# Late heads' pair parts, a third low part and the second norm's adds in other places

## What is computed

```
h = rms_norm(x);  z = h @ w_in     # pool 512 | q 512 | k 128 | v 128 | gate_pool 1024 | gate_attn 1024
yA = pool_mixer(z_pool) @ w_branch_pool
yB = window_attention(z_q, z_k, z_v) @ w_branch_attn
x = x + (sigmoid(gate_pool) * yA + sigmoid(gate_attn) * yB) @ w_out
h2 = rms_norm(x);  q = h2 @ w_q    # 8 heads, each with two halves of 128
s1, s2 = q_half1 . keys_1, q_half2 . keys_2       # top 16 of 128 each
cand = v1[i] + v2[j]               # top 16 of the 256 pairs, e_idx = i1 * 128 + i2
x = x + sum over the 8 * 16 chosen experts; out = rms_norm(x)
```

## Time and profile before

| | |
|---|---|
| time before, median of 3 runs | 2916.48 us (2912.46 to 2918.59) |
| the profiled execution's own time | 2923.75 us |
| its span, first to last instruction | 2921.7 us |
| mean granted TensorE clock | 0.984 of full speed |
| busy: PE, PEld, DVE, ACT, POOL | 95%, 83%, 82%, 32%, 72% |
| TensorE's wait for a weight tile's low part, whole mixer | 16.1 us in 9 waits, the longest 7.4 us |

### The profile page before, as it was taken

How to read it: one execution, slowest core, us unless ns; L and a number is a source line. 1 busy time by engine, 2 the same in 40 slices (tenths; PEclk the granted TensorE clock), 3 DMA queues, 4 the chain that set the end, 5 groups by cost and what they waited for, 6 DMA issues and landing times.

```text
span 2921.7 us, 39464 instructions
## 1 busy us (share of the span) xinstructions
PE 2785.8 (95%) x14843; PEld 2420.2 (83%) x14843; DVE 2406.7 (82%) x4433; ACT 935.6 (32%) x1366; POOL 2116.6 (72%) x1542
## 2 busy tenths in 40 slices
PE   8999999989997999999999999999999999999995
PEld 6688777677887888889989988999888889988995
DVE  2622797654799995889999999998999999999998
ACT  4422443323322995222222222222222222222222
POOL 5444477385686997788778886888777688878885
PEclk9999999999998999999999999999999999999998
DMA  4123422123322778889989988999889799989996
GB/s 154 49 87 99 162 61 84 44 87 108 104 90 102 236 234 283 314 327 349 337 310 352 348 307 322 346 337 351 313 318 344 283 347 346 329 317 348 337 343 218
DMA packets 267725, 717.87 MB, mean 246 GB/s; under 512 B 20880, under 2 KB 104208, under 8 KB 267536
## 3 DMA queue, kind: packets, MB, share of 16 engines
q0 software_dynamic: 110912, 403.75, 36.8%
q1 hardware_dynamic: 156624, 311.61, 31.7%
HBM read 657.86 MB, written 57.41 MB: 245 GB/s over the span
## 4 chain that ended last, share of the span: by engine, by line
DVE 20%; PE 20%; DMA 7%; issue 7%; POOL 5%; ACT 1%; DVEq 0%; POOLq 0%; SPq 0%; ACTq 0%
DVE acc L1883 9%; DVE e_y L1939 4%; DMA up<-in_down,e_idx 4%; PE ybank L1728 3%; PE abank L1712 3%; PE abank L1713 3%; PE abank L1714 3%; PE ybank L1729 3%; PE ybank L1730 3%; DVE up L1871 3%; DMA up<-in_up,e_idx 3%; POOL tdown_lo L1660 2%; DVE w_lo L1932 2%; POOL up L1653 2%; DVE w L1928 2%
## 5 line engine op out<-in xcount | busy, mean ns | idle before, releaser
L1712 PE MATMUL abank<-m_hT,tdown_hi 128*128 128x384 f32 (+1 forms) x1856 | 577.3, 311 | 4.7 <-PEq L1359 2.5
L1714 PE MATMUL abank<-m_hT,tdown_lo 128*128 128x384 f32 (+1 forms) x1856 | 577.5, 311 | 0.0
L1713 PE MATMUL abank<-m_hlo,tdown_hi 128*128 128x384 f32 (+1 forms) x1856 | 576.7, 311 | 0.0
L1728 PE MATMUL ybank<-tup_hi,w_hi 128*128 128x512 f32 x1280 | 506.8, 396 | 46.4 <-DVE e_y L1939 29.0
L941 POOL TENSOR_TENSOR m_wlo<-m_raw,m_whi 128x1024 fp32r<-128x1024 f32 x128 | 312.4, 2448 | 306.7 <-ACT m_whi L719 303.2
L1883 DVE SCALAR_TENSOR_TENSOR acc<-up,e_act,acc 128x1024 f32<-128x1024 f32 x381 | 489.5, 1285 | 43.7 <-DMA up<-in_up,e_idx 16.4
L1871 DVE CUSTOM_DVE_ANT_0 up<-up,acc 128x1024 f32<-128x1024 f32 x384 | 453.1, 1212 | 71.7 <-DMA up<-in_down,e_idx 62.4
L1729 PE MATMUL ybank<-tup_lo,w_hi 128*128 128x512 f32 x1280 | 504.5, 394 | 0.0
L1730 PE MATMUL ybank<-tup_hi,w_lo 128*128 128x512 f32 x1280 | 504.1, 394 | 0.0
L1653 POOL DMA_INDIRECT up<-in_up,e_idx x384 | 396.6, 1033 | 106.7 <-issue 88.9
L1653 POOL DMA_INDIRECT up<-in_down,e_idx x384 | 402.3, 1048 | 98.0 <-issue 73.7
(11 more groups left out here) (241 smaller groups left out, 4566.9 us busy)
## 6 DMA issues: line engine op xcount, KB each, us to landing
e_tup<-in_up SPq DMA_DIRECT2D x128, 512.0 KB
m_raw<-in_tiles SPq DMA_DIRECT2D x116, 512.0 KB, 3.5
e_tdown<-in_downT SPq DMA_DIRECT2D x116, 512.0 KB
gates<-all_table SPq DMA_DIRECT2D x64, 640.0 KB
all_table<-t_out SPq DMA_DIRECT2D x9, 4096.0 KB, 14.7
m_raw<-in_downT SPq DMA_DIRECT2D x12, 512.0 KB, 3.7
up<-in_down,e_idx POOLq DMA_INDIRECT x384
up<-in_up,e_idx POOLq DMA_INDIRECT x384
```

The lines of the kernel that those rows point to most:

```text
L1712: nc.tensor.matmul(out, tdown_hi[:, q, at], h2T_hi[:, k, a:b], start=k == 0, stop=False)
L1713: nc.tensor.matmul(out, tdown_hi[:, q, at], h2T_lo[:, a:b, at], start=False, stop=False)
L1714: ins = nc.tensor.matmul(out, tdown_lo[:, q, at], h2T_hi[:, k, a:b], start=False, stop=k == KD - 1)
L1728: nc.tensor.matmul(out, w_hi[r][:, q, ts], tup_hi[r][:, q, ds], start=q == 0, stop=False)
```

## The change

It is one of order alone: no computation is added or dropped.

- In the merge, `top_pairs` of a late head comes ahead of block m's low part (now `merge_low(m)`), except at m = 0. Heads 6 and 7 move from m = 3 and 5 to m = 4 and 6. `LOOKUPS` has one lookup for each m; the last one, (7, 1), comes behind the merge and the low parts of "out" 2 to 4.
- On GpSimd, at the end of the first group, the low part of the second group's third tile comes ahead of head 3's lookups, the fourth's between the two, the fifth's inside the second one, behind its multiply.
- In the second norm, of both groups, VectorE's adds of blocks 1, 2 and 3 move ahead of norm steps of the blocks before them.

```diff
-LATE = {0: 4, 2: 5, 3: 6, 5: 7}
+LATE = {0: 4, 2: 5, 4: 6, 6: 7}
-LOOKUPS = {1: ((4, 0),), 2: ((4, 1),), 3: ((5, 0), (5, 1)), 4: ((6, 0),), 5: ((6, 1),), 6: ((7, 0),), 7: ((7, 1),)}
+LOOKUPS = {1: (4, 0), 2: (4, 1), 3: (5, 0), 4: (5, 1), 5: (6, 0), 6: (6, 1), 7: (7, 0)}
...
-            def choose(g, hd, i):
+            def choose(g, hd, i, between=None):
...
                 link(nc.gpsimd.tensor_tensor(hit, hit, itopf[:, i].unsqueeze(2)
                                              .to_broadcast([P, TT, TOPK, TOPK]), ALU.mult))
+                if between is not None:
+                    tile_low(between)
                 for n in (8, 4, 2, 1):
...
                     if g and m in LOOKUPS:
-                        for hd, i in LOOKUPS[m]:
-                            choose(g - 1, hd, i)
+                        choose(g - 1, *LOOKUPS[m])
...
+                if g:
+                    through("out", 4)
+                    choose(g - 1, PH - 1, 1)
                 through("pq", 2)
...
-                    for hd in range(FIRST_LATE):
+                    for hd in range(FIRST_LATE - 1):
                         choose(g, hd, 0)
                         tile_low(min(first + NTILE + RING, made[0] + 1))
                         choose(g, hd, 1)
                         tile_low(min(first + NTILE + RING, made[0] + 2))
+
+                    tile_low(first + NTILE + RING)
+                    choose(g, FIRST_LATE - 1, 0)
+                    tile_low(first + NTILE + RING + 1)
+                    choose(g, FIRST_LATE - 1, 1, between=first + NTILE + RING + 2)
...
+                def merge_low(m):
+                    dve.wait_ge(m_high, g * KD + m + 1)
+                    nc.vector.tensor_tensor(mlo[:, m], sg[:, m % 2, 0], mhi(m).bitcast(F32), ALU.subtract).then_inc(m_low, 1)
...
                     nc.vector.tensor_tensor(sg[:, m % 2, 0], sg[:, m % 2, 0], sg[:, m % 2, 1], ALU.add).then_inc(merged, 1)
-                    dve.wait_ge(m_high, g * KD + m + 1)
-                    nc.vector.tensor_tensor(mlo[:, m], sg[:, m % 2, 0], mhi(m).bitcast(F32), ALU.subtract).then_inc(m_low, 1)
+                    if m == 0:
+                        merge_low(0)
                     if g and m in LATE:
...
                         top_pairs(g - 1, LATE[m], vlate[i], ilate[i], hits_late)
+                    if m:
+                        merge_low(m)
...
-                for t in range(TT):
-                    if t:
-                        finish_norm(t - 1)
+                def add_mixed(t):
                     for n in range(2):
...
-                    norm_start(g, 1, (t,))
-                finish_norm(TT - 1)
+
+                add_mixed(0)
+                add_mixed(1)
+                norm_start(g, 1, (0,))
+                finish_norm(0)
+                norm_start(g, 1, (1,))
+                add_mixed(2)
+                finish_norm(1)
+                norm_start(g, 1, (2,))
+                finish_norm(2)
+                add_mixed(3)
+                norm_start(g, 1, (3,))
+                finish_norm(3)
```

## The result

The changed kernel takes **2899.34 us** (median of 4 runs, 2896.84 to 2901.48), where the kernel before, in 4 runs between them, took 2916.05 (2912.46 to 2918.59). The ratio is 0.9943, with a 95% interval of 0.9926 to 0.9961. The difference of the medians is 16.7 us.

What follows compares the result with a forecast made beforehand. VectorE's selection bounds the mixer and starts as early as TensorE delivers, so gaps won before 751 us count. Terms sum to -14.2, 2923.75 to about 2909.6; less 7.3 to the median, 2902 us, range 2896 to 2906.

Steps and rivals of the forecast that it cites:

- first group's norm: Second norm, first group: VectorE's adds move ahead of earlier blocks' norm steps, last scaling starts earlier: -3.1 us.
- VectorE's held operation: Last early head's tail: VectorE's L1150 must wait out GpSimd's third low part, delaying the second group's first product: +2.35 us.
- clock behind it: TensorE's clock falls behind each new wait, at the second group's first product and in the output product: +2.5 us each.
- third tile's wait: Second group's pool products: TensorE no longer waits for the third low part, made in GpSimd's idle stretch: -7.3 us.
- the merge's stall: Merge: the round of 26.35 us shrinks to 16.74 with pair parts ahead of the low part, clock included: -9.6 us.
- output tile 2's wait: Output product: TensorE's gap for a low part goes, the lookup there being over before tile 2 is wanted: -1.3 us.
- the new wait in the output product: Output product: TensorE waits for a bank freed by block 7's add, now behind head 7's pair part: +3.9 us.
- second group's norm: Second norm, second group: the same 3.0 us earlier plus 1.1 of clock: -4.1 us.
- (a): Both new waits: the clock doesn't fall there; -19.2 us, 2897; kept with the forecast, together chance 0.64.
- (b): Neither new wait arises, VectorE slips between GpSimd's operations; -25.4 us, 2891; chance 0.16.
- (c): Merge: pair part doesn't come early, a gate tile still waits once, the 9.6 stays; -4.6 us, 2912; chance 0.13.
- (d): Merge: ScalarE's sigmoid waits for the later low part, starving TensorE behind heads 5, 6 and 7; +8.3 us, 2925; chance 0.05.

Runs made afterwards that it cites:

- e1_norm: The kernel before with the second norm's new order alone: 2907.97 us, ratio 0.9965.
- e3_merge: The kernel before with the merge's part alone (pair parts ahead of the low part, heads 6 and 7 moved, one lookup a round): 2910.88 us, ratio 0.9972.
- e5_lowwait: The changed kernel with GpSimd waiting for the turned blocks' first low part before making the third low part: 2899.28 us, ratio 0.9941 to the kernel before.
- e9_after_again: The changed kernel measured again, nothing altered: 2899.87 us, ratio 0.9949 to the kernel before.
- e11_lowwait_again: Repeat of the changed kernel whose third low part on GpSimd waits for the turned blocks' first low part: 2901.00 us, ratio 0.9936 to the kernel before.
- e7_order: The kernel before with the pair part ahead of the merge's low part alone, heads and lookups at their old places: 2912.80 us, one run.
- e6_both: The changed kernel with GpSimd's third low part waiting and head 7's pair part behind the add of m = 7: 2893.73 us, ratio 0.9916 to the kernel before.
- the two halves: The kernel before with the merge part's order alone, 2912.80 us, and with its new places of heads and lookups alone, 2916.17 us.
- e2_third: The kernel before with the third, fourth and fifth low parts moved alone: 2911.07 us, ratio 0.9972.
- e4_head7: The changed kernel with head 7's pair part at m = 7, its lookups behind out 3 and out 7: 2898.50 us, ratio 0.9934 to the kernel before.

## Why the prediction was right, step by step

The forecast was 2902, the measurement 2899.34. The mechanism of each term was seen, with one exception that the sum didn't need, the cause of the old stall in the merge (below). The sizes, at points that both traces have (the first group's transposes 299.32 and 299.11, the second group's first product, the copies behind pool products 0 and 3, the high copies behind branch products 4, 5 and 7, the second group's transposes, the first scores):

| step | predicted | measured | how it is measured |
|---|---|---|---|
| first group's norm | -3.1 | -3.25 | e1_norm alone, 122.45 to 119.20 |
| VectorE's held operation | +2.35 | +2.3 | 121.54 in the changed kernel less those 119.20 |
| clock behind it | +2.5 | +2.6 | first product 8.48 instead of 5.85 |
| third tile's wait | -7.3 | -7.3 | pool products 0 to 3, 16.72 instead of 24.04 |
| the merge's stall | -9.6 | -9.6 | round 4, 16.73 instead of 26.35 |
| output tile 2's wait | -1.3 | -1.3 | the gap of 1.27 is gone |
| the new wait in the output product | +3.9 | +3.8 | the gap of 3.82 |
| clock behind it | +2.5 | +1.5 | 49.92 less 3.82, against 44.56 without the wait |
| second group's norm | -4.1 | -3.9 | transposes to first scores, 26.72 instead of 30.65 |
| sum | -14.2 | -15.5 | first scores 751.47 and 736.00 |

The measured terms make -15.2, and 0.2 lie ahead of them (the start of the first transposes). The difference of the medians, 16.7, is 1.3 more than the traces show, which no step explains and which its interval (some 11 to 22 us) covers. The term that was mis-sized is **the clock behind the wait in the output product**. I had taken it near the two falls that the kernel before shows, 3.0 and 2.2; it measured 1.5: the matmuls behind the gap took 0.39 each until 668.8, 0.63 until 672, and 0.39 again. Behind the same gap it came to 1.6, 1.5 and 1.4 in `e3_merge`, `e5_lowwait` and `e9_after_again`, and to 2.6 in `e11_lowwait_again`, so the forecast lay inside what executions show.

That the other terms fit to 0.1 or 0.2 is partly luck, since they contain the clock of single traces. The first fall, +2.6 here, is 0 in the changed kernel's second trace. The third tile's wait was read as 7.3 from one trace; in `e1_norm` and `e3_merge`, which have it too, the same stretch took 25.5 instead of 24.0, so it is worth 7.3 to 8.8. And of the 3.9 of the second group's norm 0.7 is clock: with the old norm that stretch took 30.65 in the trace of before but 29.93 in `e3_merge` and `e7_order`. What the prediction got right beyond luck is each wait, its place and its length of idleness.

**The new wait, instant by instant**, from the start of round 6 (642.63). Predicted: tail free at 15.3, one-hots from 17.3, low part done at 22.1, merged at 24.8, TensorE waiting from 20.9. Measured: 657.81, 659.60, 664.76, 667.22 and 663.45, which are 15.2, 17.0, 22.1, 24.6 and 20.8. That this chain came out so close rests on one reading of the earlier trace rows, that VectorE is held while GpSimd's operation runs. The prediction's form of it, that exactly one operation is let through at the end of each, is too narrow: two got through at 655.3. The tail was free at 15.2 all the same, since it still had to wait for the end of the second low part. `e5_lowwait` took the cause away at the second group's start, and the effect with it. The Trainium skill (SBUF — State Buffer, Who interferes with whom) says that VectorE and GpSimd take a shared port pair as an exclusive lock; the trace agrees, 2.40 against 0.18.

**What would have shown it, point by point.** L1159 (L1150 before) takes 2.40 beside a third low part: seen. The wait before the second group's third product is gone: seen. Rounds of 16.74: seen, all of them. A gap of about 3.9, 4.2 us into the output product, released by the merge's add: 3.82, seen. The last norm scaling 3.6 behind the start of the transposes: 302.60 less 299.11 is 3.5. No gap before a gate tile: none. The selection stretch, first scores to the transposes of the choice, lasts 182.22 where it lasted 182.15, so what was won before 751 was carried through.

**The rivals.** (a), that the clock doesn't fall at the new waits, is half true: it is a matter of the execution, and the changed kernel's second trace doesn't have the first of the two falls and is 2.8 us earlier behind that product, but it has one behind the second group's transposes, where 0.9 of it goes. (b), that neither wait arises, is refuted by both gaps and by the 10 us of the mixer that `e6_both` gains by removing them. (c), that the pair part doesn't come early enough, is refuted by the rounds. (d), that the sigmoid comes late and starves TensorE, was half there: ScalarE did idle for VectorE's low part, in the timeline of ScalarE

```profile
601.13 0.60 ACT L853 ACTIVATE m_sg<-bank 128x512 f32<-128x512 f32 x1 [7.64 <-DVE m_mlo L1289]
...
633.62 0.61 ACT L853 ACTIVATE m_sg<-bank 128x512 f32<-128x512 f32 x1 [6.66 <-DVE m_mlo L1289]
```

but these sigmoids start 8.7 and 7.7 us into their rounds, where I had worked out 9 and 8.5 and put the limit at 11; the low parts of the two gate tiles behind the first ran from 604.26 to 609.48, and TensorE didn't wait for either.

**What was not in the sum.** The cause of the 7.39 stall as I told it was one-sided. I put the late one-hots first and the double lookup beside them; the two halves run alone show 4.40 and 0.65 left, so it was above all the double lookup. The sum didn't depend on it, since the change removes both.

**Behind the mixer.** The profiled execution of before has 1979.1 us from the start of the gate table to the end, that of after 1971.7, and those of the eleven experiments, none of which touches what lies behind the mixer, 1969.0 to 1976.2. The trace of before is the longest of all. That fits with its own time lying 7.3 above its median, and so with taking the sum against it and then subtracting those 7.3 to get from the trace to a median. The kernel before has no second trace here, so that its other runs were shorter in just this stretch is inferred.

## What to carry to other kernels

When a GpSimd operation is moved into an idle stretch of its queue, look at what VectorE does in that stretch: a 0.2 us operation on SBUF was held for the whole 2.4 us of it, and in one trace of the changed kernel that cost as much again in TensorE's clock, in the other nothing. Put such fillers beside work of VectorE that isn't held, as here the low parts read from PSUM (eight in 5.36 us with and without GpSimd beside them, and `e5_lowwait`), or count the hold in. And when work moves to a later place in a queue that is in order, follow what now stands behind it to the engine that wants it last: here that was a PSUM bank's release, held up by head 7's pair part one block later than before, worth 5.4 us. The order alone had no such wait, and one block later still it was gone too, since then the pair part stood behind the add.

## What the runs showed of the hardware that I had not expected

What the clock costs behind a gap isn't fixed by the gap's length and place. Behind 3.23 to 3.26 us of idleness at one and the same place, the first product took 8.48 us in the changed kernel, 8.44 in `e2_third`, 7.30 in `e4_head7` and 5.87 in `e9_after_again`: a price of 2.6, 2.6, 1.4 and 0. Behind the gap of 1.73 or 1.74 that stands 5 to 7 us earlier the clock stayed in twelve traces, and fell in `e11_lowwait_again`, at a price of 1.67. Behind the 3.60 to 3.83 in the output product it was 1.4 to 1.6 in four traces and 2.6 in a fifth. So the idleness of such a gap can be read from one trace to within 0.1 us, what the clock adds only to within some 2.6, and that term belongs in the range rather than in the sum.
